# One step of a hybrid encoder layer: u and v rows of the experts gathered into two rings instead of one

## What is computed

```python
D_MODEL, PEER_HEADS, PEER_KEYS, PEER_TOPK = 1024, 8, 128, 16      # 128 * 128 = 16384 experts
def trunk_layer(x, c, p, ...):
    ...
    x = x + g1[:, None, :] * mix                                  # token mixers
    h2 = adaln(x, p['norm2_g'], sh2, sc2)
    x = x + g2[:, None, :] * peer(h2, p['peer_wq'], p['peer_keys'], p['peer_u'], p['peer_v'])

def block(hb):                                                    # in peer
    q = (hb @ wq).astype(jnp.float32).reshape(-1, PEER_HEADS, 2, PEER_D_KEY // 2)
    s = jnp.einsum('nhid,hikd->nhik', q, keys.astype(jnp.float32))
    top_s, top_i = lax.top_k(s, PEER_TOPK)
    ...                                                           # 16 x 16 candidates a head, the best 16 of them
    ue = u_tab[eidx]
    ve = v_tab[eidx]
    act = jax.nn.gelu(jnp.einsum('nhkd,nd->nhk', ue, hb).astype(jnp.float32))
    return jnp.einsum('nhk,nhkd->nd', (g * act).astype(ve.dtype), ve)
```

## Time and profile before

| | us |
|---|---|
| median of 3 runs (lowest, highest) | 3894.31 (3892.48, 3895.02) |
| the profiled execution | 3893.3 |
| its span, first to last instruction | 3891.6 |

### The profile page before, as it was taken

How to read it: one execution, slowest core, us unless ns; L and a number is a source line. 1 busy time by engine, 2 the same in 40 slices (tenths; PEclk the granted TensorE clock), 3 DMA queues, 4 the chain that set the end, 5 groups by cost and what they waited for, 6 DMA issues and landing times.

```text
span 3891.6 us, 30579 instructions
## 1 busy us (share of the span) xinstructions
PE 3200.9 (82%) x9335; PEld 1509.3 (39%) x9335; DVE 2134.9 (55%) x4835; ACT 1125.9 (29%) x3428; POOL 1419.1 (36%) x1112
## 2 busy tenths in 40 slices
PE   8899999998787977887797787779779777877776
PEld 1566666666422422332242233233224223322222
DVE  0343333433467576567557656755765675675444
ACT  1123222233323222322322332332223223232222
POOL 0000000000135355445445545544553554455553
PEclk9789999999799999999999999999999999999999
DMA  8400010002289999999999999999999999999998
GB/s 280 162 19 19 19 35 19 19 14 113 113 326 419 378 422 421 408 387 422 417 378 421 422 393 404 421 418 378 421 421 366 419 421 415 374 421 421 421 422 357
DMA packets 195498, 1218.85 MB, mean 313 GB/s; under 512 B 34785, under 2 KB 35745, under 8 KB 54817
## 3 DMA queue, kind: packets, MB, share of 16 engines
q0 software_dynamic: 156672, 1140.92, 71.6%
q1 hardware_dynamic: 38688, 76.34, 5.6%
HBM read 1205.68 MB, written 11.50 MB: 313 GB/s over the span
## 4 chain that ended last, share of the span: by engine, by line
DMA 36%; PE 20%; issue 7%; DVE 5%; ACT 5%; POOL 3%; POOLq 0%; PEldq 0%; ACTq 0%
DMA shared<-in_uv,eidx_even 19%; DMA shared<-in_uv,eidx_odd 16%; PE bank L952 12%; PE bank L940 6%; DVE shared L1167 4%; POOL shared L914 3%; ACT wt L1030 1%; ACT dg L1034 1%; DMA x_even<-xmid 1%; PE bank L963 1%; DMA x_odd<-xmid 1%; ACT ge L1027 1%; PE bank L922 0%; ACT L1027 0%; ACT L1000 0%
## 5 line engine op out<-in xcount | busy, mean ns | idle before, releaser
L952 PE MATMUL bank<-shared,dg 128*128 128x512 f32 (+1 forms) x4352 | 2023.1, 610 | 604.6 <-ACT dg L1034 604.5
L952 PEld LDWEIGHTS bank<-shared,dg 128*128 128x128 f32 (+1 forms) x4352 | 789.2, 189 | 1822.7 <-ACT dg L1034 946.9
L914 POOL DMA_INDIRECT shared<-in_uv,eidx_even x576 | 743.7, 1291 | 848.3 <-PE bank L952 649.4
L1167 DVE CUSTOM_DVE_ANT_0 shared<-shared,h_even 128x1024 f32<-128x1024 f32 x576 | 704.4, 1225 | 572.7 <-DMA shared<-in_uv,eidx_even 571.4
L914 POOL DMA_INDIRECT shared<-in_uv,eidx_odd x512 | 666.3, 1301 | 660.1 <-PE bank L952 578.6
L1167 DVE CUSTOM_DVE_ANT_0 shared<-shared,h_odd 128x1024 f32<-128x1024 f32 x512 | 626.9, 1224 | 482.9 <-DMA shared<-in_uv,eidx_odd 482.1
L1027 ACT ACTIVATE ge<-dots 128x2 f32<-128x2 f32 x544 | 110.0, 202 | 1662.3 <-DVE dots L1167 1662.1
L1034 ACT ACTIVATE dg<-ident,wt 128x128 f32<-128x128 f32 x1024 | 355.3, 394 | 16.7
L906 POOL IOTA iota<- 128x16 f32 x1 | 0.1, 144 | 939.9 <-POOLq L116 939.9
L940 PE MATMUL bank<-wk,h2T 128*128 128x512 f32 x576 | 257.9, 593 | 0.0
L343 PE MATMUL bank<-shared,hT 128*128 128x512 f32 (+3 forms) x576 | 221.1, 545 | 0.0
(11 more groups left out here) (272 smaller groups left out, 2123.6 us busy)
## 6 DMA issues: line engine op xcount, KB each, us to landing
wout<-in_w_ada SPq DMA_DIRECT2D x12, 2048.0 KB, 8.1
shared<-in_w_in SPq DMA_DIRECT2D x1, 10288.0 KB, 33.6
shared<-in_uv,eidx_even POOLq DMA_INDIRECT x576, 12.1
shared<-in_uv,eidx_odd POOLq DMA_INDIRECT x512, 12.1
wout<-in_w_out SPq DMA_DIRECT2D x1, 4096.0 KB, 28.8
xn<-in_x_prompt SPq DMA_DIRECT2D x8, 512.0 KB, 4.7
xt<-in_x_prompt SPq DMA_DIRECT2D x8, 512.0 KB, 4.0
xmid<-mix SPq DMA_DIRECT2D x8, 512.0 KB, 2.9
```

What stands on the lines that cost most here:

```text
L914: pool.indirect_dma_start(ring[:, k % RING, :], None, a["uv"], bass.IndirectOffsetOnAxis(flat(eidxs[n % 2][:, :, :])[:, k:k + 1], 0)).then ...
L952: mm = pe.matmul(bank[SUM_BANK(n) + c][0:T, :], dg[:, k % RING, 0:T], ring[:, k % RING, DM + 512 * c:DM + 512 * c + 512], start=(k == 0), ...
L1167: ins = dve.tensor_tensor_reduce(ring[:, sl, 0:DM], ring[:, sl, 0:DM], h2s[n % 2][:, :], 1.0, 0.0, ALU.mult, ALU.add, dots[:, k:k + 1])
```

## The change

The ring of eight slots of 8 KB becomes two rings in the same 64 KB a partition: `uring` with six slots of 4 KB and `vring` with ten. The table is read as 32768 rows of 4 KB, u at row 2e and v at row 2e + 1. POOL issues two gathers a slot, u first. Slots of the rings and of `dg` (still eight, now `DGS`) go by the running number g = `BEFORE(n)` + k. A u gather waits until the dots of the batch are done that holds slot g - 6; a v gather until the matmuls of slot g - 10 are done. ACT now waits for the matmuls of slot g - 8 before it writes `dg`; PE waits for the landing of v as well as for `dg`. DVE makes two index tiles (`ur`, `vr`).

```diff
-RING = 8
+URING, VRING, DGS = 6, 10, 8
...
+            table = a["uv"].rearrange("e (i d) -> (e i) d", i=2)
...
-                        pool.wait_ge(sem("slot_free"), BEFORE(n) + k + 1)
+                        g = BEFORE(n) + k
+                        if g >= URING:
+                            pool.wait_ge(sem("dots"), (g - URING) // BATCH + 1)
+                        else:
+                            pool.wait_ge(sem("slot_free"), VRING)
                         pool.sem_inc(sem("pool_fence"), 1)
-                        pool.indirect_dma_start(ring[:, k % RING, :], None, a["uv"], bass.IndirectOffsetOnAxis(flat(eidxs[n % 2][:, :, :])[:, k:k + 1], 0)).then_inc(sem(f"landed{k % RING}"), 16)
+                        pool.indirect_dma_start(uring[:, g % URING, :], None, table, bass.IndirectOffsetOnAxis(flat(ur[n % 2][:, :, :])[:, k:k + 1], 0)).then_inc(sem(f"u_in{g % URING}"), 16)
+                        pool.wait_ge(sem("slot_free"), g + 1)
+                        pool.sem_inc(sem("pool_fence"), 1)
+                        pool.indirect_dma_start(vring[:, g % VRING, :], None, table, bass.IndirectOffsetOnAxis(flat(vr_[n % 2][:, :, :])[:, k:k + 1], 0)).then_inc(sem(f"v_in{g % VRING}"), 16)
...
-                        pe.wait_ge(sem("dg"), BEFORE(n) + k + 1)
+                        g = BEFORE(n) + k
+                        pe.wait_ge(sem(f"v_in{g % VRING}"), (g // VRING + 1) * 16)
+                        pe.wait_ge(sem("dg"), g + 1)
...
-                pe.sem_inc(sem("slot_free"), RING)
+                pe.sem_inc(sem("slot_free"), VRING)
...
-                        act.activation(dg[:, k % RING, 0:T], token[:, 0:T], ACT.Copy, scale=wt[:, k:k + 1]).then_inc(sem("dg"), 1)
+                        g = BEFORE(n) + k
+                        if g >= DGS:
+                            act.wait_ge(sem("slot_free"), VRING + g - DGS + 1)
+                        act.activation(dg[:, g % DGS, 0:T], token[:, 0:T], ACT.Copy, scale=wt[:, k:k + 1]).then_inc(sem("dg"), 1)
...
-                        dve.scalar_tensor_tensor(eidxs[n % 2][:, 0:hn], e1[:, 0:hn], float(PK), e2[:, 0:hn], ALU.mult, ALU.add).then_inc(sem("routed"), 1)
+                        own.mark(dve.scalar_tensor_tensor(e1[:, 0:hn], e1[:, 0:hn], float(PK), e2[:, 0:hn], ALU.mult, ALU.add))
+                        own.after()
+                        dve.tensor_scalar(ur[n % 2][:, 0:hn], e1[:, 0:hn], 2.0, None, ALU.mult)
+                        dve.tensor_scalar(vr_[n % 2][:, 0:hn], e1[:, 0:hn], 2.0, 1.0, ALU.mult, ALU.add).then_inc(sem("routed"), 1)
...
+                    if n and j == 0:
+                        dve.wait_ge(sem("dg"), BEFORE(n - 1) + (FINISH_AT + 1) * BATCH)
                     for k in range(j * BATCH, (j + 1) * BATCH):
-                        sl = k % RING
-                        dve.wait_ge(sem(f"landed{sl}"), (BEFORE(n) // RING + k // RING + 1) * 16)
-                        ins = dve.tensor_tensor_reduce(ring[:, sl, 0:DM], ring[:, sl, 0:DM], h2s[n % 2][:, :], 1.0, 0.0, ALU.mult, ALU.add, dots[:, k:k + 1])
+                        g = BEFORE(n) + k
+                        sl = g % URING
+                        dve.wait_ge(sem(f"u_in{sl}"), (g // URING + 1) * 16)
+                        ins = dve.tensor_tensor_reduce(uring[:, sl, :], uring[:, sl, :], h2s[n % 2][:, :], 1.0, 0.0, ALU.mult, ALU.add, dots[:, k:k + 1])
```

More of the change, by code:

```diff
@@ L820, in sp_ @@
                 return PB.enter_context(nc.sbuf_tensor(name, shape, dt))
-            ring = shared[:, 0:RING * 2 * DM].rearrange("p (a n) -> p a n", a=RING)
+            uring = shared[:, 0:URING * DM].rearrange("p (a n) -> p a n", a=URING)
+            vring = shared[:, URING * DM:(URING + VRING) * DM].rearrange("p (a n) -> p a n", a=VRING)
             wk = sp_("wk", [P, KD, 2 * PH * PK])
             rows = sp_("rows", [P, 4, DM])
-            s, cand = shared[:, RING * 2 * DM + N_KEYS:RING * 2 * DM + 2 * N_KEYS], keysT
+            s, cand = shared[:, 2 * PH * DM + N_KEYS:2 * PH * DM + 2 * N_KEYS], keysT
             xs = [sp_("x_even", [P, DM]), sp_("x_odd", [P, DM])]
@@ L830, in build @@
             h2T = sp_("h2T", [P, KD, P])
-            dg = sp_("dg", [P, RING, P])
+            dg = sp_("dg", [P, DGS, P])
             yout = sp_("yout", [P, DM])
@@ L843, in build @@
             af, bf, e1, e2 = (sp_(m, [P, PH, TK]) for m in ("af", "bf", "e1", "e2"))
-            eidxs = [sp_("eidx_even", [P, PH, TK], U32), sp_("eidx_odd", [P, PH, TK], U32)]
+            ur = [sp_("ur_even", [P, PH, TK], U32), sp_("ur_odd", [P, PH, TK], U32)]
+            vr_ = [sp_("vr_even", [P, PH, TK], U32), sp_("vr_odd", [P, PH, TK], U32)]
+            table = a["uv"].rearrange("e (i d) -> (e i) d", i=2)
             dots, ge, wt = sp_("dots", [P, NSLOT]), sp_("ge", [P, NSLOT]), sp_("wt", [P, NSLOT])
@@ L949, in peer @@
                     for k in range(j * BATCH, (j + 1) * BATCH):
-                        pe.wait_ge(sem("dg"), BEFORE(n) + k + 1)
+                        g = BEFORE(n) + k
+                        pe.wait_ge(sem(f"v_in{g % VRING}"), (g // VRING + 1) * 16)
+                        pe.wait_ge(sem("dg"), g + 1)
                         for c in range(2):
-                            mm = pe.matmul(bank[SUM_BANK(n) + c][0:T, :], dg[:, k % RING, 0:T], ring[:, k % RING, DM + 512 * c:DM + 512 * c + 512],
+                            mm = pe.matmul(bank[SUM_BANK(n) + c][0:T, :], dg[:, g % DGS, 0:T], vring[:, g % VRING, 512 * c:512 * c + 512],
                                            start=(k == 0), stop=(k == SLOTS(n) - 1))
@@ L1173, in finish @@
                     ci = 0 if n else 1
-                    dve.wait_ge(sem("slot_free"), BEFORE(n) + SLOTS(n) + RING)
+                    dve.wait_ge(sem("slot_free"), BEFORE(n) + SLOTS(n) + VRING)
                     prev(dve, sem("y_stored"), n * 16)
```

## The result

The changed kernel takes 4036.7 us (median of 4 runs, 4033.9 to 4061.0) against 3894.1: a ratio of 1.038, 95% interval 1.034 to 1.042. It is slower, as forecast, and by 143 us, not by 379. The profiled execution took 4034.0 us with a span of 4032.2.

The account below looks back on a forecast made before the run. POOL's issuing of 2176 gathers was to replace the transfers as bound: 1042.7 before the gathers + 2698 issues + 479 dots + 35 long products + 16 end = 4270.7 us of span, so 4273 us, 9.7% slower; range 3990 to 4640.

Parts of the forecast that it names:

- the rule read from the kernel before: A POOL issue that starts inside a two-input DVE operation finishes 0.80 us after that operation ends; all but three fit.
- Bytes a slot: DMA engines in the gather stage: still 1 MB a slot, between 2.485 and about 2.65 us, taken as 2.57.
- Start: First 100 us of the gather stage: more slots ahead could fill idle DMA, at most 21 us; taken as 0.
- The waits for dots: POOL's u gathers waiting for the dots of the batch holding the slot six back: covered, nothing added.
- End: From the last issue to the end of the kernel: 16 us with an empty queue, where it was 24.3.
- delays of POOL by the dots: Gather stage: 1088 dots at random phase each delay a POOL issue by 0.44 us, 479 us in all.
- the long products: Five DVE products of 2.29 us a tile delay POOL's issues: 35 us in all, between 0 and 70.
- The waits for slots: POOL's gathers waiting for ring slots to come free in the gather stage: nothing added.
- lower lock, or DMA as bound: Gather stage: u pattern nearly always, 4009 us, or packets cost 2.65 us a slot, 3944; 3900 to 4053, chance 0.15.
- The pattern worked out for the u gathers: Dots always delay a u issue on POOL: 2.71 us a slot, delay 0.23 a slot, 250 us in all.
- Faster: Rival: POOL isn't the bound, DMA engines set the pace: 3858 us, 0.9% faster; chance 0.06 of over 0.2% faster.
- threshold of 2.598 us a slot: Slot time that decides the faster rival: POOL may lose at most 0.12 us a slot to delays over 2.48.

Follow-up runs that it names:

- all three cures: The changed kernel with gathers ordered u, u, v, v, VectorE's long products in four pieces and the scoring matmuls spread over every second batch: 3904.4 us.
- the spread of the scoring: The kernel before with the next tile's scoring matmuls behind every second batch in place of eight batches in a row: 3831.3 us, ratio 0.984.

## Why the prediction was right and wrong

**Right.** POOL takes the place of the transfers as what the chain goes through; a free gather of 4 KB costs 0.94 and 0.30 us, and 2176 of them 2698 us; DVE's two-input operations delay POOL's gathers by the rule read from the kernel before, which all but six of the 2176 rows follow. Bytes a slot: 2.57 us was taken, 2.56 measured. Start: nothing was gained, as taken; tile 1 begins 12.3 us later than before (1235.6 for 1223.3). The waits for dots: nothing (4.3 us). End: 16 us taken, 18.5 measured.

**Wrong: the term "delays of POOL by the dots".** It stood at 479 us, with 35 for the long products, 514 in all; measured were 231, of which the dots made 193. The waits for slots, put at nothing, were 42 us; the long products, taken at 35, were 40. Put into the sum, with the end as measured, this gives 1042.4 + 2698 + 231 + 42 + 18.5 = 4032, the span. What failed is the step that took the dots' phase as random and the queue of transfers as empty. The first dot of the changed kernel does begin 3.4 us after the end of its gather's issue, as worked out for an empty queue:

```profile
1042.40 1.09 POOL L922 DMA_INDIRECT shared<-in_uv,ur_even  x1 [92.82 <-PEq L991]
...
1046.86 1.23 DVE L1189 CUSTOM_DVE_ANT_0 shared<-shared,h_even 128x1024 f32<-128x1024 f32 x1 [4.64 <-DMA shared<-in_uv,ur_even]
```

But the third begins after 5.1 and the median of all after 5.6. From issue to landing all u gathers (L922) take

```profile
DMA to landing us min/median/max: 4.3/6.6/10.6
```

and not 4 to 5, since POOL's 2.48 us a slot lie below the 2.56 that the transfers need. The run with 2 KB rows, where the queue is empty, had 0.51 us a slot of delays and 4336 us. That this is near the 0.47 of the forecast is luck, since nearly all of it falls on v gathers, by a fixed pattern.

**The rivals.** The time lies in the range of 3990 to 4640, near its lower end, and in the band of "lower lock, or DMA as bound" (3900 to 4053, a chance of 0.15), and its second half says why, if not how: the two limits, 2.48 us of POOL and 2.56 of the transfers, lie so near each other that POOL is held in step by the transfers in calm stretches (by the reading above), and falls out of it at the long products and after the scoring. The pattern worked out for the u gathers isn't what holds: the calm rows show v gathers delayed, by 0.08 us, and over the stage the u gathers have 77 us of the delays and the v gathers 154. That its 2.71 us a slot are near the measured 2.73 is luck. "Faster" was off: the packets alone cost 2.56 - 2.485 = 0.075 us a slot, 82 us, and with all three cures 3904 stayed above 3894. (Its threshold of 2.598 us a slot doesn't come out of its own sum, which gives (3894 - 1042.7 - 18.7)/1088 = 2.603; nothing hangs on it.)

**A gain that the forecast left out.** The ten slots of v save 52 us and the early release of u 15. I had looked at the new waits only for what they cost. The kernel before lost (2.596 - 2.485) x 1088 = 121 us against its own best pace. Of these the spread of the scoring gives back 63.

The account of the 147 us: packets 82; the kernel before was 121 over its pace of 2.485, the changed one is (2.731 - 2.56) x 1088 = 186 over its own, 65 more.

**Signs.** Forecast for the middle tiles were a share of 0.85 to 0.9 and 355 to 370 GB/s; the share stayed at 1.00 to 1.01, at 382 to 395 GB/s in tiles 1 to 7. The row named as the sign of packets as the bound, a share of 0.99, was no sign of either.

## What to carry to other kernels

Before a transfer is cut in two, count the issues on the engine that makes them: a gather of 128 rows cost 1.24 us of POOL whether its rows had 2, 4 or 8 KB, and delays that one issue a slot had hidden were paid in full at two. Where two limits lie within a few per cent of each other, don't take the phase between them as random and don't take it as free: look at which of them keeps a queue, and at what empties it. And where a queue runs dry in a certain stretch, first try to spread the work that stops it; here one line gave 63 us, against 143 lost by more buffers that were paid for with more issues.

## What was not expected of the hardware

- Gathers of half the bytes made the kernel 300 us slower (4336 against 4037), with 0.51 us of delays a slot in place of 0.21: with earlier landings nearly every dot falls on a v gather.
- Gathers of 4 KB rows reach 409 GB/s and of 8 KB rows 422, 3% apart, though a load of 4 KB rows by SyncE ran at 416 beside one of 10 KB rows at 408.
- A DMA share of 1.00 to 1.03 stands for anything from 384 to 422 GB/s.
- A two-input product of VectorE delays a gather only if it has begun before the gather; the gather then ends 0.80 us after the product. The Trainium skill, SBUF — State Buffer, section "Who interferes with whom", has the contention but infers that such products leave the making of descriptors alone; 0.97 us at 1511.59 speaks against that.
